# Second feed-forward of a two-block transformer kernel: quarter products of sums for all gate and value columns, three sums by adding transfers

## What is computed

```python
h2 = rms_norm_2(x, g_ffn[i])
x = x + (jax.nn.silu(h2 @ w_gate[i]) * (h2 @ w_up[i])) @ w_down[i]
```

## Time and profile before

| | us |
|---|---|
| median of 3 runs | 2475.56 |
| profiled execution, its own time | 2475.75 |
| its span, first to last instruction | 2473.6 |
| TensorE busy | 2467.2 |
| VectorE busy | 1845.7 |
| ScalarE busy | 1244.1 |
| second feed-forward's stretch, about | 1634 to 2340 |

### The profile page before, as it was taken

The page is one execution under the profiler, slowest core; times in us unless marked ns, Lnnn a source line. Parts: engine busy times, 40 slices in busy tenths (PEclk is TensorE's granted clock), DMA queues, the critical chain, the costliest instruction groups (busy, mean ns, idle before and its releaser), DMA issues.

```text
span 2473.6 us, 30290 instructions
## 1 busy us (share of the span) xinstructions
PE 2467.2 (100%) x11922; PEld 2068.6 (84%) x11922; DVE 1845.7 (75%) x1466; ACT 1244.1 (50%) x1118; POOL 41.0 (2%) x56
## 2 busy tenths in 40 slices
PE   9999999999999999999999999999999999999999
PEld 9988888888888888888888888888888888888887
DVE  5556555899999999986676656557888888888765
ACT  5344444655555555556544443345555555555553
POOL 0000000000000000000000000000000000000000
PEclk9999999999999999999999999999999999999999
DMA  8545455565555555554655555556655555655543
GB/s 283 187 151 175 153 204 187 197 212 204 194 187 196 190 200 203 192 212 152 217 186 189 169 192 184 205 186 211 212 193 200 196 195 202 203 203 194 213 157 121
DMA packets 238396, 476.72 MB, mean 193 GB/s; under 512 B 10006, under 2 KB 11094, under 8 KB 237542
## 3 DMA queue, kind: packets, MB, share of 16 engines
q1 hardware_dynamic: 234678, 460.25, 55.0%
q0 software_dynamic: 3600, 15.25, 1.8%
q10 hardware_dynamic: 32, 0.01, 0.0%
HBM read 471.28 MB, written 4.19 MB: 192 GB/s over the span
## 4 chain that ended last, share of the span: by engine, by line
PE 98%; DVE 1%; issue 0%; ACT 0%; DVEq 0%; ACTq 0%
PE acc L2005 53%; PE acc L2264 7%; PE acc L2266 7%; PE acc L2265 7%; PE acc L1998 6%; PE aux L2264 5%; PE aux L2266 5%; PE aux L2265 5%; PE aux L2051 1%; PE aux L2333 1%; PE aux L2457 0%; PE aux L2133 0%; PE aux L2114 0%; PE acc L2072 0%; PE aux L2214 0%
## 5 line engine op out<-in xcount | busy, mean ns | idle before, releaser
L2005 PE MATMUL acc<-w_hi,act_hi 128*128 128x512 f32 x1932 | 757.9, 392 | 0.0
L2005 PE MATMUL acc<-w_hi,act_lo 128*128 128x512 f32 x1932 | 752.4, 389 | 0.0
L2005 PE MATMUL acc<-w_lo,act_hi 128*128 128x512 f32 x1932 | 751.9, 389 | 0.0
L1169 DVE TENSOR_TENSOR w_lo<-raw,w_hi 128x2048 fp32r<-128x2048 f32 (+1 forms) x191 | 426.7, 2236 | 289.4 <-ACT w_hi L727 289.4
L727 ACT ACTIVATE w_hi<-raw 128x2048 fp32r<-128x2048 f32 (+1 forms) x191 | 357.3, 1871 | 546.8 <-PE acc L2005 468.9
L743 ACT ACTIVATE w_hi<-mem 128x2048 fp32r<-128x2048 f32 x168 | 322.1, 1917 | 256.0 <-PE aux L2266 147.1
L2005 PEld LDWEIGHTS acc<-w_hi,act_lo 128*128 128x128 f32 x1932 | 362.6, 188 | 76.1
L2005 PEld LDWEIGHTS acc<-w_hi,act_hi 128*128 128x128 f32 x1932 | 362.7, 188 | 75.9 <-issue 2.3
L1175 DVE TENSOR_TENSOR w_lo<-mem,w_hi 128x2048 fp32r<-128x2048 f32 x168 | 384.3, 2289 | 54.0 <-ACT w_hi L743 53.4
L2005 PEld LDWEIGHTS acc<-w_lo,act_hi 128*128 128x128 f32 x1932 | 362.9, 188 | 73.4
L737 ACT ACTIVATE w_hi<-raw 128x2048 fp32r<-128x2048 f32 x140 | 268.4, 1918 | 303.8 <-PE acc L2005 161.1
(11 more groups left out here) (201 smaller groups left out, 2124.1 us busy)
## 6 DMA issues: line engine op xcount, KB each, us to landing
raw<-in_w_in SPq DMA_DIRECT2D x103, 1024.0 KB, 5.1
raw<-in_w_ffn_up SPq DMA_DIRECT2D x48, 1024.0 KB, 5.2
mem<-in_w_ffn_down SPq DMA_DIRECT2D x44, 1024.0 KB, 5.2
mem<-in_w_down SPq DMA_DIRECT2D x44, 1024.0 KB, 5.0
mem<-in_w_ffn_up SPq DMA_DIRECT2D x40, 1024.0 KB, 5.0
raw<-in_w_ple_gate SPq DMA_DIRECT2D x32, 1024.0 KB, 5.5
raw<-in_w_gate SPq DMA_DIRECT2D x24, 1024.0 KB, 5.3
raw<-in_w_up SPq DMA_DIRECT2D x24, 1024.0 KB, 5.3
```

The source lines that it names most:

```text
L1169: v.tensor_tensor(w_lo[:, u % SPL, 0:c], raw[:, r % RAW, 0:c], w_hi[:, u % SPL, 0:c], ALU.subtract).then_inc(lo_done, 1)
L2005: mm = pe.matmul(acc[:, s, m, 0:width], x[:, k, c], w, start=start and n == 0, stop=stop and n == 2, skip_group_check=True)
```

## The change

- All four row blocks of gate and value go through Winograd's scheme: blocks 0 and 1 are set "a", 2 and 3 are set "b". A round has 14 half units and 4 down units, 18 steps. Products of the sets accumulate in the same PSUM banks.
- Weight sums: per round 8, of which VectorE makes 5 (`second_sum` a and b, `third_sum` a and b, `next_sum`), and GpSimd's queue makes 3 by transfers with an add (`add_onto`: weights from HBM are added onto what lies in the buffer): onto B22b, onto B12a of the next round, onto B22a. `p4b`, `p5a` and `p4a` wait for these (`added_f4`, `added_f1`).
- Loads on SyncE: 12 of 1 MB per round as before, 6 quarters and 6 singles in two buffers.
- The down products no longer pass VectorE: ScalarE writes x into the PSUM banks first (`seed`), the matmuls add onto it, ScalarE copies it back (`down_read`). Partial sums are kept in gate0 and gate1 in PSUM, which ScalarE fills by a copy (`part_to`). `gate_out` and `pair_out` become `value_out` (2 of 128 x 512) and a `silu` from PSUM.
- In the head: token sums for two sets (`token_sums2` twice, each one 2048 and four 512 wide) and two matmuls that open the `high` banks.

The core of the diff:

```diff
-                 ["p5", "p1", GATE2, "p6", GATE3, "p7", DOWN[0], "p2", DOWN[1], "p4", "p3", VALUE2, VALUE3, DOWN[2], DOWN[3]]]
+                 ["p5a", "p5b", "p1a", "p1b", DOWN[0], "p3a", "p3b", "p2a", DOWN[1], "p6a", "p6b", "p2b", DOWN[2], "p7b", "p7a",
+                  DOWN[3], "p4b", "p4a"]]
...
+        SINGLES = [DOWN[0], "p2a", DOWN[1], "p2b", DOWN[2], DOWN[3]] + LAST
...
+            def load_two(i, more):
...
+                single(2, DOWN[0], i)
+                single(3, "p2a", i)
+                single(4, DOWN[1], i)
+                fixed("B12a", "p6a")
+                fixed("B12b", "p6b")
+                single(5, "p2b", i)
+                if more:
+                    single(6, DOWN[2], i + 1)
+                fixed("B11b", "p7b")
+                fixed("B11a", "p7a")
+                if more:
+                    single(7, DOWN[3], i + 1)
+                fixed("B22b", "p4b")
+                fixed("B22a", "p4a")
...
+            def split_two(i, s):
...
+                elif x == "p5a" and not first:
+                    act.wait_ge(added_f1, times(i, 16, 0))
...
+                elif x[:2] == "p4":
+                    act.wait_ge(added_f4["ab".index(x[2])], times(i, 16, 16))
...
+                act.wait_ge(unit_used, times(i, PER[1], u - SPL + 1))
+                act.activation(w_hi[:, u % SPL, :], two_buf(x), ACT.Copy).then_inc(hi_done, 1)
...
+                def between(i, j, ends):
+
+                    if j == 1:
+                        f_split(1, i)
+                        part_to(i, "p5b", val_tok[:, 1, :], cross, scale=neg_r[:, 1:2])
                     if j == 2:
+                        act.wait_ge(f_done, times(i, 1, FS + 1))
+                        seed(1, low, None if isinstance(i, int) and i == 0 else times(i, 4, -2))
                     if j == 3:
+                        part_to(i, "p1b", gate0, both)
+                    if j == 5:
+                        down_read(i, 0, high)
+                        seed(2, high, times(i, 4, 1))
+                    if j == 9:
+                        down_read(i, 1, low)
+                        if not ends:
+                            seed(3, low, times(i, 4, 2))
+                    if j == 10:
+                        part_to(i, "p6b", val_tok[:, 0, :], both, scale=neg_r[:, 0:1])
+                    if j == 11:
+                        silu(i, "p2b", 0)
...
+                    if j == 13:
+                        part_to(i, "p7a", gate1, both)
+                    if j == 15 and ends or j == 16 and not ends:
+                        silu(i, "p4a", 1)
...
+            def third_sum(i, h):
+
+                v.wait_ge(lo_done, ended(1, i, "p1" + h))
+                v.wait_ge(form_done[1], times(i, 5, 2))
+                v.tensor_tensor(fixed_buf("B11" + h), fixed_buf("B22" + h), fixed_buf("B11" + h),
+                                ALU.subtract).then_inc(form_done[1], 1)
...
                 def between(i, j, ends):
 
+                    if j == 1:
                         f_rest(1, i)
                     if j == 3:
+                        second_sum(i, "a")
+                    if j == 5:
+                        second_sum(i, "b")
                     if j == 7:
+                        third_sum(i, "b")
+                    if j == 9:
+                        third_sum(i, "a")
+                        value_out(i, 0, "p3b", 3)
+                    if j == 13:
+                        value_out(i, 1, "p7a", 4)
+                    if j == 14 and not ends:
+                        next_sum(i + 1)
+                    if j == 15 and ends or j == 16 and not ends:
                         pair_product(i)
...
+            def add_onto(name, kind, q, step, done):
+                slot = FIXED[name][2]
+                pool.dma_start(raw_slot(quarter_slot(1, slot), KU, N), ffn_src(1, kind, q, step),
+                               accum_op=ALU.add).then_inc(done, 16)
+
+            for i in range(PAIRS):
+                pool.wait_ge(form_done[1], 5 * i + 3)
+                pool.wait_ge(lo_done, ended(1, i, "p6b"))
+                add_onto("B22b", *QUARTER_B21["p2b"], i + 1, added_f4[1])
+                if i + 1 < PAIRS:
+                    pool.wait_ge(*fixed_in("B12a", i + 1))
+                    add_onto("B12a", "gate", 0, i + 2, added_f1)
+                pool.wait_ge(form_done[1], 5 * i + 4)
+                pool.wait_ge(lo_done, ended(1, i, "p6a"))
+                add_onto("B22a", *QUARTER_B21["p2a"], i + 1, added_f4[0])
```

More of the change, by code:

```diff
@@ new lines, in between, with round2 @@
+                    if j == 15 and ends or j == 16 and not ends:
+                        silu(i, "p4a", 1)
+                    if j == 15 and not ends or j == 17 and ends:
+                        down_read(i, 3, high if ends else low)
+                    if j == 16 and ends:
+                        f_split(1, FS - 1, KU)
+                def round2(i):
+                    for j in range(PER[1]):
+                        split_two_ahead(i, j)
+                        between(i, j, False)
+                for j in range(PER[1]):
+                    split_two_ahead(0, j)
+                    if j == 0:
+                        sums_split4(0)
+                        sums_split4(1)
+                    between(0, j, False)
@@ L1077, in ffn2 @@
                 with act.Fori(0, ROUNDS) as i:
-                    own.enter(i, [(f_hi, 1), (gate_acted, 1)], (gate_acted, i + own.n[gate_acted.num]))
+                    own.enter(i, [(f_hi, 1)], (f_hi, i + own.n[f_hi.num]))
                     round2(i + 1)
[L1080 to L1085, removed]
+                    own.leave(ROUNDS, (f_hi, own.start[f_hi.num] + ROUNDS))
@@ L1088, in ple_gate @@
+                for j in range(PER[1]):
+                    split_two_ahead(PAIRS - 1, j)
+                    between(PAIRS - 1, j, True)
             def ple_gate(g, n, b):
@@ new lines, in next_sum, with second_sum @@
+            def next_sum(i):
+                for name in ("B11b", "B12b"):
+                    v.wait_ge(*fixed_in(name, i))
+                v.tensor_tensor(fixed_buf("B12b"), fixed_buf("B12b"), fixed_buf("B11b"), ALU.add).then_inc(form_done[1], 1)
+            def second_sum(i, h):
+                v.wait_ge(lo_done, ended(1, i, "p3" + h))
+                if isinstance(i, int) and i == 0:
+                    v.wait_ge(first_formed, "ab".index(h) + 1)
+                elif h == "a":
+                    v.wait_ge(added_f1, times(i, 16, 0))
+                else:
+                    v.wait_ge(form_done[1], times(i, 5, 0))
+                v.tensor_tensor(fixed_buf("B22" + h), fixed_buf("B22" + h), fixed_buf("B12" + h), ALU.add).then_inc(form_done[1], 1)
@@ L1776, in between @@
-                    if j == 14:
-                        add_down(1, 3, high, ended(1, i, DOWN[3]), times(i, 4, 3))
-                def round2(i):
-                    for j in range(15):
-                        rest_ahead(1, i, j)
-                        between(i, j, False)
-                round2(0)
+                        third_sum(i, "b")
[4 more added lines that the diff above has]
+                        value_out(i, 1, "p7a", 4)
@@ L2478, in step2, with round2 @@
-                        mm = down_product(1, 0, u, low if q % 2 == 0 else high)
+                        pe.wait_ge(seeded, times(i, 4, n + 1))
+                        for m in range(M):
+                            mm = added_half(u, 0, n, m, DOWN_AT[n])
                     else:
-                        mm = product(1, i, x, u)
+                        mm = two(i, x, u)
                     mm.then_inc(unit_used, 1)
-                def round2(i, added):
+                def round2(i, out):
@@ L2484, in round2 @@
                     for s, x in enumerate(STEPS[1]):
                         step2(i, s, x)
[L2486 to L2487 removed]
+                        if x == "p5b":
+                            f_turn(i, out)
                 for n, (kind, q, step) in enumerate(FFN_HEAD):
```

437 lines of the change are left out of this document (314 added, 123 removed).

## The result

The changed kernel takes 2536.65 us (median of 4 runs, 2534.58 to 2539.18) against 2475.39 before: ratio 1.0248, 95% interval 1.0230 to 1.0266. The profiled execution took 2536.85 us, its span is 2535.1. The forecast was 2449, the range 2446 to 2513.

A forecast was written before the change was run, and what follows sets the result against it. TensorE's matmul count was taken as the bound: 2475.75 less 27.2 for fewer matmuls plus 0.45 for two opening matmuls gave 2449 us, the adds costing nothing; range 2446 to 2513, the forecast's own 2446 to 2456.

The forecast's parts named there:

- The matmul count: TensorE, each round: 264 matmuls instead of 276, saving 2.72 us a round, 27.2 in ten.
- the round without late transfers: Second feed-forward: a round takes 60.7 us instead of 63.43 if no transfer is late.
- step-by-step layout: Hand-written order within a round, laid out from trace prices: nothing late, three places with about 1 us of slack.
- VectorE and ScalarE fit: Each round: VectorE busy 54.2 us and ScalarE 44.1, both within 60.7.
- the price of the adding transfer: GpSimd's adds, the deciding term: one to two copies per add, with break-even at about 1.6 copies.
- the low end: GpSimd's adds cost one copy, up to 1.25: B22a's add lands between 44.0 (on time) and 47.1 (late 0.3).
- equal sharing: DMA engines: GpSimd's and SyncE's queues alternate packet for packet, as the add's packets are 2 KB too.
- the argument for the low price: Adds: GpSimd's queue had 63.9% of the time beside another load, read as more than an equal share.
- D3's load: SyncE's queue, each round: issued at 29.9, needed by 40.4, the only load called near its need.
- The rule cited above from the Trainium skill: DMA engines: a reducing transfer reads two sources, so runs at half a copy's rate; would make the change a loss.
- Rival 1: B22a's add late for p4a's split: 2512 at two copies, chance 0.28; 2604 with two-to-one packet sharing, chance 0.06.
- Head and tail: Start and end of the kernel: extra work lies under other work and costs nothing, bounds 0 to +3 us.

The follow-up runs named there:

- run 2: The changed kernel with each adding transfer carrying a quarter of its bytes, three quarters of each sum left out: 2459.65 us.
- run 1: The changed kernel with the three adding transfers as plain copies on the same queue, sums left out: 2477.52 us.
- run 6: The changed kernel with B12a's load issued once second_sum a has used the buffer, and its add first of GpSimd's three: 2486.75 us.
- run 10: run 6 plus D3's weights loaded early into B12b's buffer, and next D0, B11a, next p2a loaded after p4b's low part: 2458.89 us, ratio 0.9933.
- run 11: run 10 with B12a's load and add back where the change had them, after p6a and between the other two adds: 2490.32 us.
- run 3: The changed kernel with B12a's add issued behind B22a's on GpSimd's queue: 2532.95 us.

## Why the prediction was wrong, point by point

**What held.** The matmul count and the round without late transfers: 60.73 us in run 2 against 60.7. The step-by-step layout too. VectorE's timeline of the changed kernel has `third_sum` b, p2b's low part and `third_sum` a:

```profile
2019.74 2.28 DVE L1420 TENSOR_TENSOR mem<-raw,mem 128x2048 f32<-128x2048 f32 x1
2021.94 2.28 DVE L1431 TENSOR_TENSOR w_lo<-mem,w_hi 128x2048 fp32r<-128x2048 f32 x1
...
2026.73 2.28 DVE L1420 TENSOR_TENSOR raw<-raw 128x2048 f32<-128x2048 f32 x1
```

With p5b's end at 1994.42 (there `f_turn` begins in the chain of work) they end at 27.6, 29.8 and 34.6; the prediction had 27.7, 29.9 and 34.7. VectorE and ScalarE fit, at 55 and 46 us.

**The step that failed** is the price of the adding transfer: "I take the low end up to 1.25 copies (47.1, late 0.3)". It is 1.9 copies alone and 1.8 in company. The reason given was that GpSimd's queue had 63.9% of the time in the earlier trace rows, which are headed "both queues full". They were not. In the trace of the kernel before, SyncE's load was issued at 1599.83, and the queues show, from 1600 to 1603 us and from 1604 to 1606:

```profile
1599.83 0.37 SPq L597 DMA_DIRECT2D raw<-in_w_o  x1
```

```profile
q0 software_dynamic: 154, 1.26, 99.8%
...
q1 hardware_dynamic: 374, 0.77, 100.1%
q0 software_dynamic: 14, 0.03, 4.1%
```

GpSimd's queue had the engines to itself, then SyncE's; they met for about 1 us. The 63.9% say nothing of how two full queues share, nor of an add's price. With 2 KB packets on both sides the count is 398 to 400, so the equal sharing that I took for the layout was right, and the argument for the low price contradicted it. What these rows do show was passed over: SyncE's load had its first packets between 1603 and 1603.7 us, 3.2 to 3.9 us after its issue, the lateness that D3's load had later. The rule cited above from the Trainium skill, which spoke for two copies, was the better evidence. (The 47.1 itself is off: between the landings at one copy, 44.0, and at 1.5, 48.6, a straight line gives 46.3.)

**Rival 1** (B22a's add late) was the right mechanism and named the right place. Its layout at two copies has B22a landing 18.4 us after issue; it landed after 19.7 in the mean. Its time of 2512 is 25 us too small. It counts ten rounds of 67.0 us. Nine measured rounds are 69.1 in the mean, 19 us more, of which the later landing explains 1.3 us in each; all that lies outside these nine came to 12 us, not the 6 of the tenth round. Head and tail had been costed at 0 to +3 us: run 2, whose rounds are exact, is at 2459.65 and not at 2448.4, 11 us more. Of that the waits show 6.7 us (two in the head, 1.3 and 1.8; two in the tail, 2.6 behind `f_rest` and 1.0 behind the copy of a partial sum). The mean clock around them is 0.97 from 1700 to 1760 us and 0.96 from 2310 to 2350, by which I estimate 3.4 us more. The last microsecond I did not isolate.

**D3's load** was named as near its need and given no landing. It landed by 43.4 (ScalarE's start at 2037.84), needed by 40.4. In the change this lateness cost nothing of its own, since B22a's add came later still; what the load costs there is the share of the engines that it takes from the adds. Its lateness comes out when the adds are early or cheap: in run 1 D3's load is on the chain of five rounds, in run 6 of seven.

**The loss by runs.** 2536.65 - 2475.17 = 61.5 us is: matmuls -26.8 (by count); head, tail and what quarter adds cost +11.2 (run 2); copies of full size on a second queue, which make D3 late, +17.9 (run 1 less run 2); the adds against copies, in price and in packet size, +59.1 (the change less run 1). These are differences of runs and not costs that stand side by side, since a round waits for the one transfer that is latest: moving B12a's add and load gave 50, moving the loads of D3, B12b and three more after that gave 28 (run 10), while the second move without the first gave 46 (run 11).

## What to carry to other kernels

An adding transfer is not free work off the engines: count it as about two copies on the DMA engines, and look at the stretch between its issue and its need, not at the mean share of the round (0.77 here, and yet the add landed 7 to 9 us late). Before moving sums to it, list every transfer due in that stretch with its own deadline, the plain loads too, and put what can move where the engines idle. Moving one add with its load, D3's and B12b's loads and three others turned 61 us of loss into 16 of gain, with the same sums by the same transfers. When several waits show up in a round, follow the chain before pricing them: the longest of TensorE's waits here, that for D3, was not what the round waited for. And before a row serves as evidence for how two queues share, check microsecond by microsecond that both were at work.

## What the runs showed of the hardware

- An adding transfer from HBM onto SBUF in 2 KB packets: 206 GB/s alone with the engines full (2026 to 2028 us of the change), against 392 for copies and 381 for plain copies on the same queue in 4 KB packets (run 1); 8 us per MB beside a stream of copies. GpSimd's issue of 1 MB takes 1.27 us for an add in 2 KB packets, 0.84 for a quarter of it (run 2), 0.75 for a plain copy in 4 KB packets (run 1).
- Two queues with work share the engines packet for packet: 398 to 400 for 2 KB packets on both sides, 63 to 65 for 4 KB beside 2 KB (run 1, 1815 to 1816 us).
- A load issued on SyncE's queue while GpSimd's queue has the engines to itself sent its first packets about 4 us later: 3.9 to 4.2 us in the change, and 3.2 to 3.9 us in the kernel before. I had not expected that; why is open.
- After 3.35 us idle TensorE's granted clock fell to its lower level, with matmuls 0.43 us apart, and eight of them cost 1.6 us more. Whether that counts depends on the chain: nothing in the change, some 13 us in run 3.
